# Opening loads of a fused decoder layer: x of three tiles and the first weights on one DMA queue

## The reference

```python
def _rmsnorm(x, g):
    x32 = x.astype(jnp.float32)
    y = x32 * lax.rsqrt(jnp.mean(x32 * x32, axis=-1, keepdims=True) + EPS)
    return (y * g.astype(jnp.float32)).astype(x.dtype)

def _swiglu(x, wg, wu, wd):
    return (jax.nn.silu(x @ wg) * (x @ wu)) @ wd

...
        h = h + 0.5 * _swiglu(_rmsnorm(h, ffn1_norm[l]), ffn1_wg[l], ffn1_wu[l], ffn1_wd[l])
        h = h + _mixer(h, mem, positions, ...)
        h = h + 0.5 * _swiglu(_rmsnorm(h, ffn2_norm[l]), ffn2_wg[l], ffn2_wu[l], ffn2_wd[l])
    return _rmsnorm(h, final_norm)
```

## Time and profile before

| | us |
|---|---|
| median of 3 runs | 1685.51 |
| lowest and highest of them | 1684.53, 1949.92 |
| the profiled execution, its own time | 1683.99 |
| its span on the slowest core, core 4 | 1682.9 |
| its spans on the eight cores | 1674.2 to 1682.9 |

### The profile page before, as it was taken

How to read it: one execution, slowest core, us unless ns; L and a number is a source line. 1 busy time by engine, 2 the same in 40 slices (tenths; PEclk the granted TensorE clock), 3 DMA queues, 4 the chain that set the end, 5 groups by cost and what they waited for, 6 DMA issues and landing times.

```text
span 1682.9 us, 24190 instructions; the slowest of 8 cores (1674.2 to 1682.9 us)
## 1 busy us (share of the span) xinstructions
PE 1623.9 (96%) x7819; PEld 750.0 (45%) x7819; DVE 870.0 (52%) x1474; ACT 728.5 (43%) x1172; POOL 121.1 (7%) x228
## 2 busy tenths in 40 slices
PE   7999999999999999999999999999999999999996
PEld 2445444434444444444444444454444444444442
DVE  6662442435764566654565544654654464433344
ACT  5213001046862256952477862378983221210113
POOL 0102011100000000000000000000000011001000
PEclk9999999999999999999999999999999999999998
DMA  8769998776564475454987774976444454522212
GB/s 212 107 114 124 146 121 117 121 163 191 120 139 156 147 162 115 107 145 153 263 202 179 170 185 160 266 212 161 128 167 144 157 168 153 164 80 89 78 35 100
DMA packets 78889, 249.10 MB, mean 148 GB/s; under 512 B 9440, under 2 KB 11760, under 8 KB 78320
## 3 DMA queue, kind: packets, MB, share of 16 engines
q0 software_dynamic: 28864, 107.49, 35.3%
q1 hardware_dynamic: 49904, 140.06, 25.7%
HBM read 282.91 MB, written 54.00 MB: 200 GB/s over the span
## 4 chain that ended last, share of the span: by engine, by line
PE 91%; DVE 3%; ACT 3%; issue 2%; DMA 1%; SPq 0%; DVEq 0%; ACTq 0%
PE ps_all L562 91%; ACT mb L588 1%; DVE hS L600 1%; ACT ma L588 1%; DMA ring<-wb 1%; ACT L588 1%; DMA hS<-x 1%; DVE ntm L600 0%; DVE mb L595 0%; ACT fa L588 0%; DVE aF L595 0%; DVE gU L600 0%; ACT B L611 0%; DVE ma L595 0%; DVE ma L600 0%
## 5 line engine op out<-in xcount | busy, mean ns | idle before, releaser
L562 PE MATMUL ps_all<-ntm,ring 128*128 128x512 bf16 x2224 | 528.6, 380 | 5.3 <-ACT ma L588 2.2
L562 PE MATMUL ps_all<-B,ring 128*128 128x512 bf16 x2016 | 450.2, 379 | 2.3 <-DVE gU L600 0.9
L562 PEld LDWEIGHTS ps_all<-ntm,ring 128*128 128x128 bf16 x2224 | 215.9, 98 | 265.0 <-issue 15.1
L588 ACT ACTIVATE fa<-ps_all 128x512 f32<-128x512 f32 x170 | 101.4, 598 | 468.3 <-PE ps_all L562 460.1
L562 PEld LDWEIGHTS ps_all<-B,ring 128*128 128x128 bf16 x2016 | 196.1, 98 | 236.7 <-issue 6.8
L562 PE MATMUL ps_all<-aF,ring 128*128 128x512 bf16 x1232 | 296.0, 382 | 2.6 <-DVE hS L600 1.7
L600 DVE SCALAR_TENSOR_TENSOR hS<-ps_all,hS 128x512 f32<-128x512 f32 x248 | 168.7, 689 | 101.5 <-PE ps_all L562 101.0
L595 DVE TENSOR_TENSOR aF<-fa,ps_all 128x512 bf16<-128x512 f32 x148 | 101.4, 687 | 225.5 <-PE ps_all L562 219.2
L562 PEld LDWEIGHTS ps_all<-aF,ring 128*128 128x128 bf16 x1232 | 120.7, 98 | 150.1 <-issue 11.2
L588 ACT ACTIVATE mb<-ps_all 128x512 bf16<-128x512 f32 (+1 forms) x304 | 161.3, 575 | 37.6 <-PE ps_all L562 34.6
L588 ACT ACTIVATE ma<-ps_all,hv 128x512 f32<-128x512 f32 x104 | 71.2, 687 | 183.2 <-PE ps_all L562 162.3
(11 more groups left out here) (129 smaller groups left out, 1213.5 us busy)
## 6 DMA issues: line engine op xcount, KB each, us to landing
ring<-wb SPq DMA_DIRECT2D x112, 512.0 KB, 4.2
ring<-f1g POOLq DMA_DIRECT2D x44, 512.0 KB, 9.7
ring<-f2bg POOLq DMA_DIRECT2D x44, 512.0 KB, 3.6
wb<-wm POOLq DMA_DIRECT2D x28, 512.0 KB, 13.4
ma<-spill SPq DMA_DIRECT2D x48, 256.0 KB, 4.4
ring<-wb SPq DMA_DIRECT2D x48, 256.0 KB, 3.8
ring<-f2g POOLq DMA_DIRECT2D x22, 512.0 KB, 7.8
f2bg<-ring SPq DMA_DIRECT2D x22, 512.0 KB, 5.8
```

The costliest lines, as they stand in the source:

```text
L562: i = e.matmul(_ap(o), lhsT=_ap(l), rhs=_ap(r), start=st, stop=sp)
L588: f.add([("act", lambda e: e.activation(out=_ap(out), in_=_ap(in_), func=func, scale=_ap(scale), **kw), c_act(out, bias is not None))], ou ...
```

## The change

All twelve transfers of x of tiles 0, 1 and 2 move from SP's queue to POOL's. The loads of x of tiles 1 and 2, and their copies, squares and norm factors, are no longer written ahead of the first SwiGLU half but inside its first group, through two new entries of `OPENING` behind (2, 0); `arrive(t)` is the body of the old loop with the load of x ahead of it. The five waits that were added by hand, the list `first` and the `after` argument are gone. `vecs` stays on SP, where it is now the first transfer. On POOL's queue this gives, in the order of the program: x of tile 0, three weight tiles, x of tile 1, x of tile 2, two more weight tiles, the down weights.

```diff
-OPENING = [(0, 0), (1, 0), (2, 0), (0, 1), (1, 1), ...
+OPENING = [(0, 0), (1, 0), (2, 0), ("x", 1), ("x", 2), (0, 1), (1, 1), ...
...
-        op = f.dma("pool", t[:, 0:n], src[:, 0:n], nbytes=128 * n * (2 if isinstance(src, (T, R)) else 4))
-        if first is not None:
-            first.append(op)
+        f.dma("pool", t[:, 0:n], src[:, 0:n], nbytes=128 * n * (2 if isinstance(src, (T, R)) else 4))
...
-    def load_x(t, slot, after=None):
-        ops = []
+    def load_x(t, slot, q="sp"):
         for c in range(0, 8, 2):
-            op = f.dma("sp", R(hslot[slot][c], hAP[slot][:, c:c + 2, :]),
-                       x_d[t][:, c * TT:(c + 2) * TT].rearrange("p (c n) -> p c n", c=2),
-                       outs=[hslot[slot][c + 1]], nbytes=524288, after=after)
-            ops.append(op)
-        return ops
-
-    x0 = load_x(0, 0)
+            f.dma(q, R(hslot[slot][c], hAP[slot][:, c:c + 2, :]),
+                  x_d[t][:, c * TT:(c + 2) * TT].rearrange("p (c n) -> p c n", c=2),
+                  outs=[hslot[slot][c + 1]], nbytes=524288)
+
+    load_x(0, 0, "pool")
     f.dma("sp", vecs, vecs_d, nbytes=128 * NV * 4)
-    x1 = load_x(1, 1)
-    x2 = load_x(2, 2)
-    first = []
...
             for at, (j, i) in enumerate(todo):
+                if j == "x":
+                    arrive(i)
+                    continue
...
     raws = []
-    for t in range(2):
+
+    def arrive(t):
+        if t:
+            load_x(t, t, "pool")
+        if t == 2:
+            rmsnorm(hslot[2], [vcol(V_F1 + c) for c in range(8)], D, nB[2], banks="n")
+            return
         p = bank("n")
...
         raws.append((raw_at[t], r))
-    rmsnorm(hslot[2], [vcol(V_F1 + c) for c in range(8)], D, nB[2], banks="n")
+
+    arrive(0)
...
     epoch[0] = 2
-    first[0].deps.add(x0[1].seq)
-    for op in x1:
-        op.deps.add(first[0].seq)
-    for op in x2:
-        op.deps.add(first[2].seq)
-    first[3].deps.add(x1[2].seq)
-    first[4].deps.add(x2[2].seq)
```

More of the change, by code:

```diff
@@ L445 @@
 LATER = 1000000
-OPENING = [(0, 0), (1, 0), (2, 0), (0, 1), (1, 1), (2, 1), (3, 0), (3, 1), (0, 2), (1, 2), (2, 2), (3, 2), (4, 0), (4, 1), (4, 2)]
+OPENING = [(0, 0), (1, 0), (2, 0), ("x", 1), ("x", 2), (0, 1), (1, 1), (2, 1), (3, 0), (3, 1), (0, 2), (1, 2), (2, 2), (3, 2), (4, 0), (4, 1), (4, 2)]
 MB = {}
```

## The result

The changed kernel takes 1689.1 us (median of 15 executions) against 1685.4 us for the kernel before, measured beside it. The ratio is 1.0018 with a 95% interval of 1.0011 to 1.0025, so it is about 3 us slower. That is far inside 2%, but on the other side of the forecast of 1683.9. Some executions of either kernel run with one die at a lower clock, up to 1980 us; the ratios and means here leave them out.

The account below looks back on a forecast made before the run. TensorE was taken to bound the kernel, busy 1623.9 of 1682.9 us. The terms -2.0 + 0.9 + 0 = -1.1 took 1683.99 to 1682.9; 1.0 added for the other runs gave 1683.9, range 1680 to 1689.

Parts of the forecast that it names:

- The pause in the transfers goes: -2.0.: Opening, core 4: nothing moves from 10.4 to 12.4 us between x and weights; this falls away, -2.0 us.
- S: Theory of the experiments, not the prediction: memory is shared, a neighbour uses what one core's pause leaves; no chance given.
- x starts 0.9 us later: +0.9.: Opening: POOL takes 2.7 us from issue to moving data, SP 1.85, so x starts later, +0.9 us.
- x moves no slower once it has started: Opening: the same DMA engines move x after its start, so POOL's queue should make it no slower.
- The order of the work: I take 0.: Tiles 1 and 2: lower priority for squares and copies most likely leaves the same plan, shifted, since PE is full; 0.
- The bound of 4 us: 200 to 600 us: a new order moving a third of PE's 12.1 us waiting would be 4 us, up or down.
- Whatever the first weight tile gains is gained by the whole kernel.: Opening: PE has no hole from 17.01 to 77.5 us, so the gain carries through if nothing arrives too late behind.
- The slowest core: Whole kernel: the slowest core sets the time, so core 4 is followed; cores differ by 8.7 us.
- It does nothing: Rival, opening: POOL's start as slow as on core 4, pause as short as on core 5; +0.1, 1685; chance 0.13.
- The new order costs: Rival, elsewhere in the kernel: the new order of all engines costs 4 us, 1687.9; chance 0.10.
- The clock did rise earlier: Rival, first 16 matmuls: a shorter wait lets the higher clock level come sooner, -1.7 us more, 1682.2; chance 0.12.
- Late descriptors beside the memsets of va: Rival, opening: DVE's memsets shut POOL out, x starts at 9.5 us; +4.6 in sum, 1689.6; chance 0.07.

Follow-up runs that it names:

- a2: Kernel before with only tile 0's x moved to POOL's queue, all waits kept; ratio 1.0029, and 1.0023 once more.
- a3: Kernel before with tile 0's x on POOL's queue and the first weight tile no longer waiting for x; ratio 1.0027.
- g1: Kernel before with the first weight tile waiting for the first transfer of tile 0's x instead of the second; ratio 1.0005.
- i1: Kernel before with its own transfers and waits, but copies, squares and norm factors of tiles 1 and 2 at the change's late priority; ratio 1.0015.
- k1: Kernel before with its first weight tile loaded in two halves, gate and up; ratio 1.0000.
- l1: The change's transfers under the old work order, but tile 0's x on SP and the first weight tile waiting for its second piece; ratio to before 0.9998.
- the repeated run: The changed kernel itself, measured again later beside the kernel before; ratio 1.0019.
- the two halves: Kernel before with the change's new work order alone, and kernel before with the change's transfers alone; ratio 1.0015 each.
- g2: Kernel before with the first weight tile waiting for nothing and the second for the third transfer of tile 0's x; ratio 1.0055.

## Why the prediction was wrong, step by step

Two terms of the sum failed. The missing pause, put at -2.0, was worth 0.6 us in bytes and was lost again before the first matmul. The new order of the work, put at 0, cost 1.6 us.

**"The pause in the transfers goes: -2.0."** This is the step that failed first. The pause went, but in the mean over the cores the 2.62 MB were moved only 0.6 us sooner without it (a2 to a3: 14.95 to 14.38; before to g1: 14.28 to 13.71). Core 4 had the long pause; the prediction's own rows give core 5 one of 0.8. And even the 0.6 us didn't reach the first matmul, which started about 0.9 us later behind these bytes than with the pause (2.2 to 2.4 us after them and not 1.3 to 1.5). One might read the stretch from 8 to 17 us as the gain, 1.89 MB a core against 1.63. But a2, which keeps the pause, has 1.80 there: that is late x, and the missing pause adds 0.05 (1.85 in a3).

The other explanation, S, is that its neighbour uses what one core's pause leaves. It isn't shown. The Trainium skill, "HBM Reference" (Specifications (TRN2)), says that the two cores of a domain share its bandwidth. In the kernel before, each pair of neighbouring cores (0 and 1, 2 and 3, and so on) had one core at 285 to 291 GB/s and one at 203 to 209 from 2 to 8 us, which looks like sharing. But their 500 GB/s were no limit of the pair. From 26 to 30 us, when x of tiles 1 and 2 moves, cores 4 and 5 had 339 + 406 = 745:

```profile
26.00:30.00 4.00, 4.00 (x20) 1.82 (x19) 3.56 (x8) 2.71 (x5) 0.00 (x0) 1.00 0.97 339
...
26.00:30.00 4.00, 4.00 (x21) 1.80 (x19) 3.73 (x9) 3.13 (x7) 0.58 (x1) 1.00 1.00 406
```

**"x starts 0.9 us later: +0.9."** This was right in size. POOL's first issue didn't fall where SP's did, at 1.06: it fell at 1.58, after 0.89 us of idle. In the mean over the cores the first 1.0 MB were moved 0.8 us later than through SP (7.36 in a2 against 6.53) and 2.10 MB, all of x, 0.7 us later (11.05 against 10.34). So the sentence that x moves no slower once it has started also stands; the 0.28 MB that a core with x on POOL is behind at 8 us are the late start. The Trainium skill, "DMA: Bandwidth & Descriptors" (Issuing engine by pattern), which the prediction weighed and which puts plain loads on the Sync queue, was right in sign: a2 is slower with x on POOL's queue, by 1.0029 and 1.0023.

**The bytes were counted as if they moved in order.** This is the likeliest place of the other 0.9 us, and the prediction has no term for it. Core 4 needed 2.10 + 0.52 = 2.62 MB for its first matmul, and by 17 us it had moved 1.16 + 1.96 = 3.12 MB. The other 0.5 MB belonged to transfers further back. In the mean a core had moved 2.88 MB when its first real matmul began before, and 3.01 after. x, too, came late: ScalarE got its last piece at 13.04, where the prediction had it moved by 11.3 and landed at about 12.3. The Trainium skill, "DMA: Bandwidth & Descriptors" (Two DMAs through the same engine are not ordered), says that within one queue of one DMA engine descriptors only start in order, and are pipelined. The trace agrees, as far as the 0.5 MB show. That this is what makes the weights land late was not tested by itself.

For the transfers the sum is then +0.7 - 0.6 + 0.9 = +1.0 at the first matmul, and 16.7 against 15.7 was measured.

**"The order of the work: I take 0."** This is the larger failure, a term put at nothing: +1.6 us at the next stage, 1.0015 in i1. The argument was that a full TensorE will follow the same plan, shifted. But TensorE was full with the copies and squares of tile 1 standing early on VectorE and ScalarE. The change puts them behind fa and aF of three gate/up groups, and TensorE's cover is gone. For the copies it was 1.4 us: the four ox copies were made by 28.60 + 0.88 = 29.48, and the first matmul that reads them started at 30.92. What TensorE then waited for were the squares: five sums stand ahead of that matmul after the change, and ScalarE, idle for 1.59 us until an fa came, made the fourth square from 30.25. The bound of 4 us that stood beside it, from the waits between 200 and 600 us, was wide enough, but it looked in the wrong place: 30 us, not 200.

**"Whatever the first weight tile gains is gained by the whole kernel."** It fell with k1: 0.8 us earlier, nothing gained. Three of the cores wait for the next weight, a copy or a square, and the first 16 matmuls take longer.

**The slowest core.** The prediction followed core 4, which did as little as 0.05 us better, and named as its last risk that core 5's opening might lose. This is what happened: 14.39 to 17.21. But core 5 was early before by luck: in other kernels with x on SP it started at 16.45 (i1) and 17.21 (l1). The prediction took one execution's late and early core for fixed; the mean over the cores, 15.7 to 16.7, is what the change did.

**The rivals.** "It does nothing" (1685) came nearest in its mechanism, the pause given back by the start. Its price of +0.1 is also what these two terms come to, 0.7 - 0.6; it missed the later landing. (Its 1684.99 leaves the +0.1 out; with it the sum is 1685.09.) "The new order costs", 1687.9, had the right sign, and it was one of the two causes; it measured 1.6 us at the next stage where the bound was 4. The clock did rise earlier on core 4: its first 16 matmuls took 22.28 - 16.96 = 5.32 us and not 6.36. Over the eight cores they took 5.87 against 5.55, so there was no such gain. Late descriptors beside the memsets of va: data moved at 258 GB/s by 4 to 5 us, ahead of the 4.9 that the rival needed, and of the 0.8 us that x is late 0.52 are POOL's later issue.

**What was right:** no pause, x of tile 1 in time (VectorE's ox copies don't wait for a transfer), no wait for the fourth weight tile, and no price for the number of issues (l1). That vecs at the head of SP's queue costs nothing was not tested: it stands there in every kernel with tile 0's x on POOL.

**The sum with measured terms**, at the next stage: transfers +1.1, order +1.6, together 2.7, as in the profile of the repeated run, and 3 us in the time. The ratios of the two halves, 1.0015 each, add up to 1.0030 where the changed kernel has 1.0018; the halves are known to 0.001 only.

## What to carry to other kernels

When a pause in one core's transfers looks like lost time, take the mean over all cores and ask two things: when have the needed bytes been moved, and how long after that does the engine start. A queue that starts later moves the first, and more transfers in flight can move the second; here they took back more than the pause gave. When a step moves work to a lower priority, look at the engine that feeds the full one: the cover is the time from its last copy to the matmul that reads it, here 1.4 us.

## What the runs showed of the hardware

- x of the first tile through POOL's queue moved 0.28 MB a core less by 8 us than through SP's, in five kernels against six (g2, with a weight tile issued at once, lies between). It is a later start and no lower rate: 1.0 MB were moved 0.8 us later, 2.10 MB 0.7 us later. The share of the DMA engines was 0.76 to 0.83 in that stretch, and 0.88 to 0.92 through SP.
- With weights issued while x was still moving, the first matmul started 2.2 to 2.4 us after a core had moved the bytes of x and one weight tile, in five kernels; with weights issued behind the landing of x's second piece, when nearly all of x had moved, 1.3 to 1.5 us after, in five others (g2 and k1 aside).
- The cores of a pair started unequally in the kernel before (203 to 209 and 285 to 291 GB/s from 2 to 8 us), and which one is ahead changes: in the two executions of a2 core 2 had its first real matmul at 17.19 and at 14.52, core 3 at 15.05 and at 18.02.
- The DMA engines were as busy on weights as on x and moved half as much by the profile's count: at a share of 1.0 some 150 to 210 GB/s and some 350. The profile counts a weight tile's 0.5 MB of bf16 (512.0 KB an issue), while 1 MB of f32 is read for it; in bytes read I estimate twice the rate, 300 to 420 GB/s. Neither the share nor GB/s alone says how fast a casting transfer goes.
- In the first profile after, all four cores of die 1 had a granted clock of 0.81 from about 30 to 46 us and those of die 0 from 29 to 34, and then 1.00 again at the same load; in the repeated run two cores had it from 29 to 33 and the others not at all. The Trainium skill, "TensorE: Matmul & The Clock Gate" (Seeing it yourself), tells of a limiter that takes a whole die to 13/16 of the clock and holds it while the load lasts. The level agrees with 0.81; that it holds doesn't, in these rows.
